# A state-space layer on one core: decay factors from running sums spread by transfers, in place of products with a triangle, and x rows turned last in their slots

## The chip, the cores and the metric

One Trainium2 chip, one of its cores. The time is that of one execution on the device, in microseconds (us); several runs are made and their median is given. Smaller is better.

## What is computed

A stack of layers on 256 positions of width 1024, float32: SwiGLU blocks, a state-space (Mamba-2) mixer, latent attention, a gated short convolution and a stick-breaking attention. The change is in the state-space mixer, which runs once. Its core, with chunks of 128 positions, 8 groups and 4 heads per group:

```python
acs = jnp.cumsum(dtc * a, axis=1)
seg = acs[:, :, None] - acs[:, None, :]
decay = jnp.exp(jnp.where(mask, seg, -jnp.inf))
cb = jnp.einsum("blgn,bsgn->blsg", cc, bc)
xdt = xc * dtc[..., None]
y_diag = jnp.einsum("blsg,blsgr,bsgrp->blgrp", cb, decay, xdt)
y_off = jnp.einsum("blgn,bgrpn->blgrp", cc, state) * jnp.exp(acs)[..., None]
decay_to_end = jnp.exp(acs[:, -1:] - acs)
```

`dt` is a softplus of a projection, `a` is negative, `xc`, `bc` and `cc` come from a projection, a causal convolution over four positions and a SiLU.

## The kernel before

The kernel is one program with a hand-written order for each of the five engines; semaphores tie them together. Every matrix product with weights is made of three products of split operands (`product`, L622 to L624: high by high, high by low, low by high, in fp32r). Weights come in units of 512 KB x 2 through a ring of four: SyncE loads `raw` (L510), ScalarE rounds it to `w_hi` (L1367), the vector engine (DVE) forms `w_lo = raw - w_hi` (L1974), and TensorE waits for `lo_ready` ahead of each unit's first product.

In the state-space layer (`mamba` of each engine) TensorE goes through 22 units of the input projection, two per step `s`, 0 to 10. Behind unit number n comes **slot n**: a batch of small work of the scan, listed by `mamba_slots(n)`. In this text slot 14, say, is the batch behind the unit of that number. Its entries, for group g:

- `dt`, `acs`: time steps; running sums of `dA = dt * a` (product with the triangle `upto`), slot 8.
- `xs` (slots 12, 14, 16, 18): a quarter of x is transposed in two turns (L639) and copied by ScalarE to `ys` (L1548).
- `cb` (from slot 12): products of B and C (L915), and for g - 2 the product of C with the carried state (L909). DVE takes `off` (L2182) and `cbm`, the masked product (L2190).
- `seg` (from slot 12): for both chunks the differences of running sums, as a product of the triangle `after_r` with `dA` spread over `upto`, in a high part `R_hi` (ScalarE, L1578, eight ACTIVATEs a group) and a low part `R_lo` (POOL, L2691). TensorE writes them to the PSUM tile `aux` (L924, L925); ScalarE takes `dend` (L1558) and the exponentials `E` (L1559); DVE multiplies E by `cbm` (L2206).
- `y` (from slot 13): E by `xdt`, eight products (L933), added to `ys` by DVE (L2211). `xdt` and `xdtd` are POOL's (L2700, L2710).
- `state` (from slot 13): B by `xdtd` (L943), copied by ScalarE (L1562).

Results of `xs`, `cb`, `y` and `state` share one PSUM tile, `tr`, with two buffers. Each use takes a **turn** number k from a common counter, and `claim_turn(k)` on TensorE waits until turn k - 2 has been read (`turn_done`, `turn_free`). A slot takes 2 turns for `xs`, 1 for `cb`, 1 for `y` and 1 for `state`. In slots with `xs`, TensorE and ScalarE do them in the order xs, seg, cb, y, state; in others cb, y, seg, state. Each engine goes through its own part of the slot in program order, then splits the next weight unit (`split_to`). ScalarE also does `first_tap` and `finish_conv` (the convolution's start and its SiLU, L1591, L1605) and DVE the rest of the convolution (`taps`, L2245), up to step 7. Exp and SiLU need different activation tables (ACT_TABLE_LOAD rows).

Of the kernel before, what the change touches and what calls it, by code (L numbers as in the profile page):

```python
# [20 lines left out]
P = 128  # L21
# [90 lines left out]
MAMBA_TURNS = {"dt": 1, "acs": 1, "btok": 1, "xs": TB, "cb": 1, "y": 2, "seg": 0, "state": 0, "g": TB}  # L112
# [52 lines left out]
def mamba_slots(n, sums_first=False):  # L165
# [11 lines left out]
    if n in (12, 14, 16, 18):  # L177
        found.append(("xs", (n - 12) // 2))
# [36 lines left out]
def program(nc, t, out):  # L215
# [4 lines left out]
    with ctx:  # L220
# [6 lines left out]
        def overlaid(*specs):  # L227
# [4 lines left out]

        raw = sb("raw", [P, RING, UNIT])
# [12 lines left out]
        after_r = sb("after_r", [P, P], F32R)  # L246
# [25 lines left out]
        BT, CT, Btok, conv, E, xdt, R_hi, R_lo, cbm, xdtd, state, dtT = overlaid(  # L272
            ("BT", [P, G, T], F32), ("CT", [P, G, T], F32), ("Btok", [P, G, P], F32),
            ("conv", [P, 4, T], F32), ("E", [P, TB, R * P], F32), ("xdt", [P, 2, TB, GW], F32),
            ("R_hi", [P, TB, R * P], F32R), ("R_lo", [P, TB, R * P], F32R), ("cbm", [P, TB, P], F32),
# [14 lines left out]
        (sz, _, ys, xsT, off, dtv, dta, dte, dt, ea, dA, dA_hi, dA_lo, eacs, dend, gss, gms, grs, sz0) = overlaid(  # L290
# [3 lines left out]
            ("dA", [P, TB, NH], F32), ("dA_hi", [P, TB, NH], F32R), ("dA_lo", [P, TB, NH], F32),  # L294
            ("eacs", [P, NH], F32), ("dend", [P, R], F32), ("gss", [P, TB, G], F32),
# [19 lines left out]
        (_, rows, after, causal, strict) = overlaid(  # L315
            ("_junk2", [P, 2 * D], F32), ("rows", [P, 4, P], F32), ("after", [P, P], F32),
# [29 lines left out]
        consts = sem("consts")  # L346
        gated = sem("gated")
# [16 lines left out]
        r_ready = sem("r_ready")  # L364
        r_hi_ready = sem("r_hi_ready")
# [38 lines left out]
        after_ready = sem("after_ready")  # L404
# [212 lines left out]
        def _(pe):  # L617
# [228 lines left out]
            def mamba():  # L846
                pe.wait_ge(consts, 9)
                pe.wait_ge(after_ready, 1)
# [28 lines left out]
                def small(n, only=None):  # L877
                    for name, g in mamba_slots(n, True):
# [1955 lines left out]
```

## Time and profile before

| | |
|---|---|
| median of 3 runs | 1298.96 us (1298.92 to 1299.41) |
| the profiled execution | 1299.49 us, its span 1297.8 us |
| TensorE busy | 1277.3 us, 98% |
| DVE, ScalarE, POOL busy | 59%, 53%, 9% |
| DMA | 219.81 MB, mean 169 GB/s |
| slots 12 to 20 of the state-space layer | 289.5 to 370.9 us of the span |

A profile row gives engine, line, operation, output and inputs by the program's names, count, and time. A product in float32 shows as two passes (x2 for one product); one in fp32r as one. "Idle before" is time that the engine stood still ahead of an instruction, with what released it. The chain of waits follows the last instruction back through whatever released it, so its pieces are time on the path. PE is TensorE, PEld its weight load, ACT ScalarE, POOL GpSimd; ACTq and SPq are the issue of DMAs on those engines.

### The profile page before, as it was taken

How to read it: one execution, taken by the hardware profiler on the slowest of the kernel's cores; microseconds unless marked ns; L12 is line 12 of the kernel's file. 1: busy time of each engine (PE TensorE's matmuls, PEld its weight loads, DVE VectorE, ACT ScalarE, POOL GpSimd, SP SyncE). 2: the span in 40 equal slices, each digit the busy share in tenths (PEclk: the TensorE clock that was granted, in tenths of full speed). 3: DMA queues.
4: the chain of work that ended last, by engine and by line, in shares of the span. 5: the costliest groups of instructions: out<-in, count | busy, mean ns of one | idle time of the engine just before them, and what ended most of it. 6: DMA issues, size and time to landing. Idle time of an engine off the chain costs nothing.

```text
span 1297.8 us, 18319 instructions
## 1 busy us (share of the span) xinstructions
PE 1277.3 (98%) x6934; PEld 1094.6 (84%) x6934; DVE 763.6 (59%) x892; ACT 682.2 (53%) x924; POOL 122.3 (9%) x198
## 2 busy tenths in 40 slices
PE   8999999999999999999999999989999999999997
PEld 7888889999888888888888888877888888999896
DVE  5655645878795655554555545765655554666654
ACT  6544435669883644443544534854644443444554
POOL 3000000008730000000000001620000000000000
PEclk9999999999999999999999999999999999999999
DMA  9656646453246466555655463412566565565431
GB/s 300 206 183 209 218 144 195 145 181 98 98 163 219 137 194 194 186 203 163 194 180 180 175 227 110 161 54 79 193 194 192 193 213 162 148 192 182 147 114 49
DMA packets 180653, 219.81 MB, mean 169 GB/s; under 512 B 8713, under 2 KB 132942, under 8 KB 180590
## 3 DMA queue, kind: packets, MB, share of 16 engines
q1 hardware_dynamic: 179614, 218.01, 51.8%
q8 instruction: 42, 0.69, 0.2%
q10 hardware_dynamic: 688, 0.79, 0.2%
q14 instruction: 21, 0.17, 0.1%
q0 software_dynamic: 288, 0.15, 0.0%
HBM read 217.87 MB, written 1.05 MB: 169 GB/s over the span
## 4 chain that ended last, share of the span: by engine, by line
PE 89%; ACT 4%; DVE 4%; issue 1%; DMA 1%; SPq 1%; POOL 1%; DVEq 0%; POOLq 0%; ACTq 0%
PE acc L622 27%; PE acc L624 27%; PE acc L623 27%; PE tr L639 4%; DVE w_lo L1974 1%; ACT w_hi L1367 1%; PE tr L933 1%; DMA raw<-in_ffn_w_up 1%; PE aux L1075 1%; PE acc L1056 1%; ACT xT_hi L1379 0%; ACT R_hi L1578 0%; ACT junk L1433 0%; SPq L510 0%; PE aux L924 0%
## 5 line engine op out<-in xcount | busy, mean ns | idle before, releaser
L1974 DVE TENSOR_TENSOR w_lo<-raw,w_hi 128x2048 fp32r<-128x2048 f32 (+2 forms) x187 | 420.4, 2275 | 176.4 <-ACT w_hi L1367 176.2
L1367 ACT ACTIVATE w_hi<-raw 128x2048 fp32r<-128x2048 f32 (+2 forms) x189 | 352.1, 1897 | 118.0 <-PE acc L624 117.2
L622 PE MATMUL acc<-w_hi,xT_hi 128*128 128x512 f32 (+1 forms) x914 | 362.4, 396 | 0.7 <-DVE w_lo L2594 0.4
L624 PE MATMUL acc<-w_hi,xT_lo 128*128 128x512 f32 (+1 forms) x914 | 355.1, 388 | 0.0
L623 PE MATMUL acc<-w_lo,xT_hi 128*128 128x512 f32 (+1 forms) x914 | 354.2, 388 | 0.0
L624 PEld LDWEIGHTS acc<-w_hi,xT_lo 128*128 128x128 f32 x914 | 171.6, 188 | 36.2
L622 PEld LDWEIGHTS acc<-w_hi,xT_hi 128*128 128x128 f32 x914 | 171.8, 188 | 35.8 <-issue 1.6
L623 PEld LDWEIGHTS acc<-w_lo,xT_hi 128*128 128x128 f32 x914 | 172.0, 188 | 33.0
L622 PE MATMUL acc<-w_hi,hT_hi 128*128 128x512 f32 x448 | 176.0, 393 | 0.4 <-DVE y_sb L2494 0.4
L624 PE MATMUL acc<-w_hi,hT_lo 128*128 128x512 f32 x448 | 174.5, 389 | 0.0
L623 PE MATMUL acc<-w_lo,hT_hi 128*128 128x512 f32 x448 | 174.4, 389 | 0.0
L622 PE MATMUL acc<-xT_hi,w_hi 128*128 128x256 f32 (+1 forms) x592 | 167.2, 283 | 1.2 <-DVE w_lo L1974 0.6
L623 PE MATMUL acc<-xT_lo,w_hi 128*128 128x256 f32 (+1 forms) x592 | 165.9, 281 | 0.0
L624 PE MATMUL acc<-xT_hi,w_lo 128*128 128x256 f32 (+1 forms) x592 | 165.9, 281 | 0.0
L2116 DVE SCALAR_TENSOR_TENSOR h<-acc,rstd,sg 128x256 f32<-128x256 f32 x88 | 38.6, 479 | 163.9 <-ACT sg L1481 163.9
L1481 ACT ACTIVATE sg<-acc,rstd 128x256 f32<-128x256 f32 x88 | 37.0, 472 | 180.1 <-PE acc L624 180.1
L622 PEld LDWEIGHTS acc<-xT_hi,w_hi 128*128 128x128 f32 (+1 forms) x592 | 112.2, 190 | 1.9 <-issue 1.7
L623 PEld LDWEIGHTS acc<-xT_lo,w_hi 128*128 128x128 f32 (+1 forms) x592 | 112.3, 190 | 0.2
L624 PEld LDWEIGHTS acc<-xT_hi,w_lo 128*128 128x128 f32 (+1 forms) x592 | 112.3, 190 | 0.0
L2666 POOL TENSOR_SCALAR mean_square<-square_sum 128x1 f32<-128x1 f32 x18 | 4.9, 275 | 1026.8 <-ACT junk L1433 567.3
L624 PEld LDWEIGHTS acc<-w_hi,hT_lo 128*128 128x128 f32 x448 | 84.1, 188 | 17.8
L622 PEld LDWEIGHTS acc<-w_hi,hT_hi 128*128 128x128 f32 x448 | 84.1, 188 | 17.7 <-DVE y_sb L2494 0.8
(298 smaller groups left out, 1160.4 us busy)
## 6 DMA issues: line engine op xcount, KB each, us to landing
raw<-in_ffn_w_down SPq DMA_DIRECT2D x88, 512.0 KB, 4.9
raw<-in_ffn_w_gate SPq DMA_DIRECT2D x86, 512.0 KB, 4.2
raw<-in_ffn_w_up SPq DMA_DIRECT2D x86, 512.0 KB, 5.2
raw<-in_ssm_w_in SPq DMA_DIRECT2D x48, 512.0 KB, 4.6
raw<-in_w_in_a SPq DMA_DIRECT2D x64, 256.0 KB, 4.1
raw<-in_ssm_w_out SPq DMA_DIRECT2D x16, 512.0 KB, 4.0
raw<-in_mla_w_out SPq DMA_DIRECT2D x8, 512.0 KB, 4.4
raw<-in_w_out_a SPq DMA_DIRECT2D x8, 512.0 KB, 5.0
```

The lines of the kernel that those rows point to most:

```text
L622: pe.matmul(o, lh, rh, start=start, stop=False, skip_group_check=skip)
L623: pe.matmul(o, lh, rl, start=False, stop=False, skip_group_check=skip)
L624: return pe.matmul(o, ll, rh, start=False, stop=stop, skip_group_check=skip)
L639: last = pe.transpose(tr[0:n, k % 2, at:at + P], src, ident[:])
L933: last = pe.matmul(tr[:, k % 2, tb * GW + r * HP:tb * GW + (r + 1) * HP], E[:, tb, r * P:(r + 1) * P], xdt[:, g % 2, tb, r * HP:(r + 1) * ...
L1056: pe.matmul(o[:, j * w:(j + 1) * w], qT[0:QK, h0 + j, tb * P:(tb + 1) * P], kT[0:QK, h0 + j, 0:w], start=j == 0, stop=False, skip_group_ch ...
L1075: last = pe.matmul(aux[:, r % 2, j * (VD + 1):(j + 1) * (VD + 1)], pT[:, r % 2, at:at + P], kv_tok[:, kb, h0 + j, NOPE:], start=kb == 0, s ...
L1367: inst = act.activation(w_hi[:, u % RING, 0:n], raw[:, u % RING, 0:n], ACT.Copy)
L1481: act.activation(sg[:, tb, :], bank(p0 + n, tb)[:, 0:CW], ACT.Silu, scale=rstd[:, tb:tb + 1]).then_inc(gated, 1)
L1974: inst = dve.tensor_tensor(w_lo[:, u % RING, 0:n], raw[:, u % RING, 0:n], w_hi[:, u % RING, 0:n].bitcast(F32), ALU.subtract)
L2116: acc_free(dve.scalar_tensor_tensor(h[:, tb, :], bank(p0 + n, tb)[:, CW:2 * CW], rstd[:, tb:tb + 1], sg[:, tb, :], ALU.mult, ALU.mult), p0 ...
L2666: link(pool.tensor_scalar(mean_square[:, b], square_sum[:, at:at + 1], 1.0 / D, EPS, ALU.mult, ALU.add))
```

## The change

`dA` no longer goes through products with a triangle. In slot 8, `acs` forms with TensorE, in one turn: the running sums of both chunks by position (128x64), the same transposed with heads on partitions (two products, 32x128), and minus the sum from a position to the chunk's end (two products, 128x32). ScalarE takes from it `eacs`, `dend` for all heads at once, `nacs` (the negated sums) and `dtT`, 32 rows of 256 sums, which it sends to DRAM (`decay_rows`, 32 KB). Per group a DMA on ScalarE's queue spreads four of the rows over all 128 partitions into one of three buffers of `E` (512 KB, `sum_rows`): groups 0 and 1 ahead of slot 10's share of the convolution, group g + 2 in slot g + 12, from g = 1 to 5 behind `y(g-1)`, which read that buffer. POOL adds the mask `future` (0 or a large negative number, `segments`), ScalarE takes eight exponentials of 128 columns with the bias `nacs`, and DVE multiplies by `cbm` as before. Precision splits of `dA`, `R_hi`, `R_lo` and the use of `aux` here are gone. `xs` stands last in its slot on all engines, so that in a slot the turns go to cb, y, state, xs, xs.

```diff
-    if n in (12, 14, 16, 18):
-        found.append(("xs", (n - 12) // 2))
...
-    for name, first in (("y", 13), ("seg", 12), ("state", 13)):
+    for name, first in (("y", 13), ("decay", 12), ("state", 13)):
         if 0 <= n - first < G:
             found.append((name, n - first))
-    if sums_first and found and found[0][0] == "xs":
-        found.sort(key=lambda slot: ("xs", "seg", "cb", "y", "state").index(slot[0]))
+    if n in (12, 14, 16, 18):
+        found.append(("xs", (n - 12) // 2))
...
+        decay_rows = nc.dram_tensor("decay_rows", (NH, T), F32).ap()
-        after_r = sb("after_r", [P, P], F32R)
+        future = sb("future", [P, P])
...
-            ("conv", [P, 4, T], F32), ("E", [P, TB, R * P], F32), ("xdt", [P, 2, TB, GW], F32),
-            ("R_hi", [P, TB, R * P], F32R), ("R_lo", [P, TB, R * P], F32R), ("cbm", [P, TB, P], F32),
+            ("conv", [P, 4, T], F32), ("E", [P, 3, R, T], F32), ("xdt", [P, 2, TB, GW], F32),
+            ("cbm", [P, TB, P], F32),
...
                         elif name == "acs":
                             pe.wait_ge(dt_dve, 2)
                             claim_turn(k)
-                            pe.matmul(tr[:, k % 2, 0:NH], upto[:], dA[:, 1, :], start=True, stop=True)\
+                            pe.matmul(tr[:, k % 2, 0:TB * NH], upto[:], dA[:].rearrange("p b n -> p (b n)"),
+                                      start=True, stop=True)
+                            for tb in range(TB):
+                                pe.matmul(tr[0:NH, k % 2, (tb + 1) * P:(tb + 2) * P], dA[:, tb, :], upto[:],
+                                          start=True, stop=True)
+                            end = tr[:, k % 2, (TB + 1) * P:(TB + 1) * P + NH]
+                            pe.matmul(end, ones[:], dA[:, 0, :], start=True, stop=False, skip_group_check=True)
+                            pe.matmul(end, upto[:], dA[:, 0, :], start=False, stop=True, skip_group_check=True)\
                                 .then_inc(turned, 1)
...
-                        elif name == "seg":
-                            for tb in range(TB):
-                                pe.wait_ge(r_hi_ready, 2 * g + tb + 1)
-                                pe.wait_ge(r_ready, 2 * g + tb + 1)
-                                if g:
-                                    pe.wait_ge(exp_done, 2 * g + tb - 1)
-                                pe.matmul(aux[:, tb, :], after_r[:], R_hi[:, tb, :], start=True, stop=False)
-                                pe.matmul(aux[:, tb, :], after_r[:], R_lo[:, tb, :], start=False, stop=True)\
-                                    .then_inc(seg_ready, 1)
...
+                def sum_rows(g):
+                    act.dma_start(E[:, g % 3, :, :].rearrange("p r t -> p (r t)"),
+                                  across(decay_rows[R * g:R * g + R, :].rearrange("r t -> (r t)"), R * T))\
+                        .then_inc(sums_landed[g % 3], 16)
...
                         if name == "acs":
                             act.wait_ge(turned, k + 1)
-                            turn_free(act.activation(eacs[:], tr[:, k % 2, 0:NH], ACT.Exp), k)
+                            act.activation(eacs[:], tr[:, k % 2, NH:2 * NH], ACT.Exp)
+                            act.activation(dend[:], tr[:, k % 2, (TB + 1) * P:(TB + 1) * P + NH], ACT.Exp, scale=-1.0)
+                            sums = tr[:, k % 2, 0:TB * NH].rearrange("p (b n) -> p b n", b=TB)
+                            act.activation(nacs[:], sums, ACT.Copy, scale=-1.0)
+                            turn_free(act.activation(dtT[0:NH, :], tr[0:NH, k % 2, P:P + T], ACT.Copy), k)
+                            turn_done(act, k)
+                            act.dma_start(decay_rows[:, :], dtT[0:NH, :]).then_inc(sums_stored, 16)
...
-                        elif name == "seg":
-                            if n in (14, 16, 18):
-                                act.wait_ge(turned, c.turn + 2)
+                        elif name == "decay":
+                            if g + 2 < G:
+                                if g:
+                                    act.wait_ge(turned, ky[0] + 1)
+                                sum_rows(g + 2)
                             for tb in range(TB):
                                 act.wait_ge(seg_ready, 2 * g + tb + 1)
-                                if tb == 0:
-                                    act.activation(dend[:], aux[:, 0, P - 1::P], ACT.Exp)
-                                act.activation(E[:, tb, :], aux[:, tb, :], ACT.Exp).then_inc(exp_done, 1)
+                                for r in range(R):
+                                    e = E[:, g % 3, r, tb * P:(tb + 1) * P]
+                                    inst = act.activation(e, e, ACT.Exp, bias=nacs[:, tb, R * g + r:R * g + r + 1])
+                                inst.then_inc(exp_done, 1)
+                        elif name == "y":
+                            ky[0] = k
...
-                def high_factors(g):
...
-                        for r in range(R):
-                            inst = act.activation(R_hi[:, tb, r * P:(r + 1) * P], upto[:], ACT.Copy,
-                                                  scale=dA_hi[:, tb, R * g + r:R * g + r + 1].bitcast(F32))
...
-                    if 6 <= s < 10:
-                        high_factors(2 * s - 11)
+                    if s == 5:
+                        act.wait_ge(sums_stored, 16)
+                        sum_rows(0)
+                        sum_rows(1)
...
-                        elif name == "seg":
...
-                                pool.tensor_tensor(
-                                    heads(R_lo[:, tb, :], R), upto[:].unsqueeze(1).to_broadcast([P, R, P]),
-                                    dA_lo[:, tb, R * g:R * g + R].unsqueeze(2).to_broadcast([P, R, P]), ALU.mult)\
-                                    .then_inc(r_ready, 1)
...
-                            pool.wait_ge(exp_done, 2 * g + 1)
...
+                def segments(g):
+                    pool.wait_ge(sums_landed[g % 3], 16 * (g // 3 + 1))
+                    for tb in range(TB):
+                        e = E[:, g % 3, :, tb * P:(tb + 1) * P]
+                        inst = pool.tensor_tensor(e, e, future[:].unsqueeze(1).to_broadcast([P, R, P]), ALU.add)
+                        inst.then_inc(seg_ready, 1)
...
                 for n in range(22):
+                    if n == 11:
+                        segments(0)
                     small(n)
+                    if 12 <= n < 11 + G:
+                        segments(n - 11)
```

TensorE, slot 14 of the input projection, before, from the second transpose of x on (`tr_read0` and `tr_read1` are the releases of the two buffers of `tr`):

```order
L639 MATMUL tr<-ident,xsT 128x128 x3
L639 MATMUL tr<-ident,xsT 128x128 [waits tr_read0]
L639 MATMUL tr<-ident,xsT 128x128 x3
L924 MATMUL aux<-R_hi,after_r 128x512 [waits exp_done,r_ready,r_hi_ready]
L925 MATMUL aux<-R_lo,after_r 128x512
L924 MATMUL aux<-R_hi,after_r 128x512 [waits exp_done,r_ready,r_hi_ready]
L925 MATMUL aux<-R_lo,after_r 128x512
L909 MATMUL tr<-state,CT 128x256 [waits tr_read0,tr_read1]
L915 MATMUL tr<-CT,BT 128x128 x2
L933 MATMUL tr<-xdt,E 128x64 [waits m_ready,xdt_ready,tr_read0]
L933 MATMUL tr<-xdt,E 128x64 x7
L943 MATMUL tr<-xdtd,Btok 128x256 [waits xdtd_ready,tr_read1]
```

The x transposes and the products into `aux` come first. TensorE, the same slot, now:

```order
L916 MATMUL tr<-state,CT 128x256 [waits tr_read0,tr_read1]
L922 MATMUL tr<-CT,BT 128x128 x2
L931 MATMUL tr<-xdt,E 128x64 [waits m_ready,xdt_ready,tr_read0]
L931 MATMUL tr<-xdt,E 128x64 x7
L941 MATMUL tr<-xdtd,Btok 128x256 [waits xdtd_ready,tr_read1]
L639 MATMUL tr<-ident,xsT 128x128 [waits tr_read0,conv_done]
L639 MATMUL tr<-ident,xsT 128x128 x3
L639 MATMUL tr<-ident,xsT 128x128 [waits tr_read1]
L639 MATMUL tr<-ident,xsT 128x128 x3
L622 MATMUL acc<-xT_hi,w_hi 128x256 [waits lo_ready]
```

The four products into `aux` are gone, and the two x turns stand behind `state`; the second waits for the release of the buffer that `state` wrote. (L909 is now L916, L915 L922, L933 L931, L943 L941.)

ScalarE, slot 14 and the split of the weight unit behind it, before:

```order
L1548 ACTIVATE ys<-tr 128x512 [waits turned] x2
L1605 ACT_TABLE_LOAD
L1605 ACTIVATE xsT<-conv 128x512 [waits acc_read2]
L1605 ACTIVATE xsT<-conv 128x512 [waits acc_read3]
L1558 ACT_TABLE_LOAD [waits seg_ready]
L1558 ACTIVATE dend<-aux 128x4 [waits turned]
L1559 ACTIVATE E<-aux 128x512
L1559 ACTIVATE E<-aux 128x512 [waits seg_ready]
L1562 ACTIVATE state<-tr 128x256 [waits turned]
L1367 ACTIVATE w_hi<-raw 128x2048 [waits unit_used,raw_landed0]
```

Here the x copies and the SiLU of the convolution come first. ScalarE, the same place, now:

```order
L1533 DMA E<-decay_rows 128x1024 [waits turned]
L1570 ACTIVATE E<-E,nacs 128x128 [waits seg_ready]
L1570 ACTIVATE E<-E,nacs 128x128 x3
L1570 ACTIVATE E<-E,nacs 128x128 [waits seg_ready]
L1570 ACTIVATE E<-E,nacs 128x128 x3
L1576 ACTIVATE state<-tr 128x256 [waits turned]
L1557 ACTIVATE ys<-tr 128x512 [waits turned] x2
L1607 ACT_TABLE_LOAD
L1607 ACTIVATE xsT<-conv 128x512 [waits acc_read2]
L1607 ACTIVATE xsT<-conv 128x512 [waits acc_read3]
L1365 ACTIVATE w_hi<-raw 128x2048 [waits unit_used,raw_landed0]
```

The copy of `state` now has a DMA issue and eight exponentials in front of it, and the x copies, `xsT` and `w_hi` come behind it.

## Rows read from the trace of the kernel before

**Rows 1.** The page's first parts: busy time of TensorE, its granted clock in 40 slices.
```profile
PE 1277.3 (98%) x6934; PEld 1094.6 (84%) x6934; DVE 763.6 (59%) x892; ACT 682.2 (53%) x924; POOL 122.3 (9%) x198
...
PEclk9999999999999999999999999999999999999999
```

**Rows 2.** The chain of waits, slot 14 and the next slot's start: start us, us, what.
```profile
306.82 0.87 PE tr L639 x8
307.70 0.23 PE aux L924
...
308.62 0.43 PE tr L909 x2
...
309.50 1.73 PE tr L933 x16
311.23 0.49 PE tr L943 x2
317.47 0.43 PE tr L909 x2
```

**Rows 3.** The tile `aux`: engine, operation, count, ns min/median/max, starts, forms.
```profile
L924 PE MATMUL aux<-R_hi,after_r x16: 393/471/497, 290.1 to 361.9; 128*128 128x512 f32 x16
```

**Rows 4.** Who waited for whom, 215 to 385 us: total, times, longest us.
```profile
PEld aux L924 <- ACT R_hi L1578: 1.8, 1, 1.8
```

**Rows 5.** The chain of waits on ScalarE ahead of slot 18, from `state`.
```profile
344.28 0.27 ACT state L1562
344.56 1.80 ACT w_hi L1367
346.36 2.32 ACT R_hi L1578 x8
```

**Rows 6.** Timeline of TensorE at `acs`: start us, us, engine, line, operation, count.
```profile
266.06 0.30 PE L893 MATMUL tr<-dA,upto 128*128 128x32 f32 x2
```

**Rows 7.** Timeline of ScalarE around slot 12.
```profile
290.93 1.15 ACT L1605 ACTIVATE xsT<-conv 128x512 f32<-128x512 f32 x2
292.10 1.28 ACT L1558 ACT_TABLE_LOAD   x1
293.39 0.17 ACT L1558 ACTIVATE dend<-aux 128x4 f32<-128x4 f32 x1
293.46 1.08 ACT L1559 ACTIVATE E<-aux 128x512 f32<-128x512 f32 x2
```

**Rows 8.** Timeline of ScalarE's queue at the program's start.
```profile
1.25 1.00 ACTq L484 DMA_DIRECT2D raw<-in_ffn_w_up  x2
```

**Rows 9.** Timeline of DVE, slots 13, 14 and 16; [idle before it <- releaser].
```profile
296.66 3.12 DVE L1974 TENSOR_TENSOR w_lo<-raw,w_hi 128x2048 fp32r<-128x2048 f32 x1
299.71 0.41 DVE L2190 TENSOR_TENSOR cbm<-tr,upto 128x256 f32<-128x256 f32 x1
...
306.64 2.28 DVE L1974 TENSOR_TENSOR w_lo<-raw,w_hi 128x2048 fp32r<-128x2048 f32 x1
309.54 0.42 DVE L2182 TENSOR_TENSOR off<-tr,eacs 128x256 f32<-128x256 f32 x1 [0.61 <-PE tr L915]
...
311.27 0.69 DVE L2211 TENSOR_TENSOR ys<-tr,ys 128x512 f32<-128x512 f32 x1 [0.33 <-PE tr L933]
...
333.20 2.55 DVE L2206 TENSOR_TENSOR E<-E,cbm 128x512 f32<-128x512 f32 x2
```

**Rows 10.** DMA issues: tensors, queue, count, KB each, us to landing.
```profile
in_gain<-in_norm_a SPq DMA_DIRECT2D x1, 512.0 KB, 7.0
f_gain<-in_norm_f SPq DMA_DIRECT2D x1, 512.0 KB, 3.8
```

**Rows 11.** Timeline of POOL, slots 13, 14 and 17.
```profile
302.75 2.04 POOL L2691 TENSOR_TENSOR R_lo<-upto,dA_lo 128x512 fp32r<-128x512 f32 x2
308.53 0.86 POOL L2700 TENSOR_TENSOR xdt<-ys,dt 128x256 f32<-128x256 f32 x1 [3.74 <-ACT ys L1548]
...
344.95 4.63 POOL L2691 TENSOR_TENSOR R_lo<-upto,dA_lo 128x512 fp32r<-128x512 f32 x2
```

More of the change, by code:

```diff
@@ L108, in unscaled @@
     return name[:3] == "ffn" or name == "mla"
-MAMBA_TURNS = {"dt": 1, "acs": 1, "btok": 1, "xs": TB, "cb": 1, "y": 2, "seg": 0, "state": 0, "g": TB}
+MAMBA_TURNS = {"dt": 1, "acs": 1, "btok": 1, "xs": TB, "cb": 1, "y": 2, "decay": 0, "state": 0, "g": TB}
 SMALLS = 16 * 9
@@ L271, in program @@
         hT_hi, hT_lo = overlaid(("hT_hi", [P, KF, T], F32R), ("hT_lo", [P, KF, T], F32R))
-        BT, CT, Btok, conv, E, xdt, R_hi, R_lo, cbm, xdtd, state, dtT = overlaid(
+        BT, CT, Btok, conv, E, xdt, cbm, xdtd, state, dtT = overlaid(
             ("BT", [P, G, T], F32), ("CT", [P, G, T], F32), ("Btok", [P, G, P], F32),
-            ("conv", [P, 4, T], F32), ("E", [P, TB, R * P], F32), ("xdt", [P, 2, TB, GW], F32),
-            ("R_hi", [P, TB, R * P], F32R), ("R_lo", [P, TB, R * P], F32R), ("cbm", [P, TB, P], F32),
+            ("conv", [P, 4, T], F32), ("E", [P, 3, R, T], F32), ("xdt", [P, 2, TB, GW], F32),
+            ("cbm", [P, TB, P], F32),
             ("xdtd", [P, GW], F32), ("state", [P, GW], F32), ("dtT", [P, T], F32))
@@ L289, in program @@
                                    ("junk", [P, D], F32), ("xn", [P, TB, D], F32))
-        (sz, _, ys, xsT, off, dtv, dta, dte, dt, ea, dA, dA_hi, dA_lo, eacs, dend, gss, gms, grs, sz0) = overlaid(
+        (sz, _, ys, xsT, off, dtv, dta, dte, dt, ea, dA, nacs, eacs, dend, gss, gms, grs, sz0) = overlaid(
             ("sz", [P, TB, 512], F32), ("_junk", [P, D], F32), ("ys", [P, TB, DI], F32),
@@ L314, in program @@
         _, in_gain = overlaid(("_g1", [P, 6 * D], F32), ("in_gain", [P, D], F32))
-        (_, rows, after, causal, strict) = overlaid(
-            ("_junk2", [P, 2 * D], F32), ("rows", [P, 4, P], F32), ("after", [P, P], F32),
+        (_, rows, causal, strict) = overlaid(
+            ("_junk2", [P, 2 * D], F32), ("rows", [P, 4, P], F32),
             ("causal", [P, P], F32), ("strict", [P, P], F32))
@@ L363, in program @@
         dt_act = sem("dt_act")
-        r_ready = sem("r_ready")
-        r_hi_ready = sem("r_hi_ready")
+        sums_copied = sem("sums_copied")
+        sums_stored = sem("sums_stored")
+        sums_landed = [sem(f"sums_landed{n}") for n in range(3)]
         seg_ready = sem("seg_ready")
@@ L877, in small @@
                 def small(n, only=None):
-                    for name, g in mamba_slots(n, True):
+                    for name, g in mamba_slots(n):
                         if only and name != only:
@@ L1939, in rotation @@
                 act.activation(causal_b[:], causal[:], ACT.Copy)
-                act.activation(strict_b[:], strict[:], ACT.Copy)
-                act.activation(after_r[:], after[:], ACT.Copy).then_inc(after_ready, 1)
+                act.activation(strict_b[:], strict[:], ACT.Copy).then_inc(masks_ready, 1)
             first_x(act, 0, 0)
@@ L2638, in _ @@
             select(from_[:], 0, 1, -1, ALU.is_ge, -1.0, 0.0)
-            select(after[:], 0, 1, -1, ALU.is_gt, 1.0, 0.0)
+            select(future[:], 0, -1, 1, ALU.is_ge, 0.0, NEG)
             pool.memset(ones[:], -1.0).then_inc(consts, 1)
@@ L2684, in small @@
                             xs_turn[g] = k
-                        elif name == "seg":
-                            if g == 0:
-                                pool.wait_ge(dt_dve, 3)
-                            for tb in range(TB):
-                                if g:
-                                    pool.wait_ge(seg_ready, 2 * g + tb - 1)
-                                pool.tensor_tensor(
-                                    heads(R_lo[:, tb, :], R), upto[:].unsqueeze(1).to_broadcast([P, R, P]),
-                                    dA_lo[:, tb, R * g:R * g + R].unsqueeze(2).to_broadcast([P, R, P]), ALU.mult)\
-                                    .then_inc(r_ready, 1)
+                        elif name == "acs":
+                            acs_turn.append(k)
                         elif name == "y":
```

34 lines of the change are left out of this document (12 added, 22 removed).

## The prediction

> **What bounds the kernel now.** I read the page first: TensorE is busy for 98% of the span, and in the 40 slices its granted clock is at the top digit throughout, the 2.4 GHz level [rows 1]. So a product taken off TensorE shortens the kernel, unless another engine's wait takes its place. The profiled run took 1299.49 us and the median of the runs is 1298.96, 0.5 lower; I make the sum against 1299.49 and take the same off the median. A measurement of this kernel tells about 0.2%, 2.6 us, from no change.
>
> Next the chain of waits through the state-space stage. Slot 14 (306.8 to 311.7 us) is TensorE without a gap [rows 2]: eight transposes of x 0.87, two pairs of `after_r` products at 0.23 each, the `cb` products 0.88 from 308.62 to 309.50, `y` 1.73, `state` 0.49. The `after_r` products are what goes. There are 16 with `R_hi` [rows 3] and, in pairs with them, 16 with `R_lo`, 32 in all. The only time in this stage when TensorE stands still is 1.8 us in slot 18, waiting for ScalarE's `R_hi` [rows 4]. Over slots 16 to 18 ScalarE is thus the late engine; what it does in its last slot before the wait is `state` 0.27, `w_hi` 1.80, eight `R_hi` 2.32 [rows 5].
>
> **The change, part by part.**
>
> Removed on TensorE: 32 products at 0.23 us on the path [rows 2, 3]: -7.4. Removed with them: the wait for `R_hi`, -1.8 [rows 4]. What is late next in slot 18 is below.
>
> Added on TensorE in `acs` (slot 8): four more products than the one of before. One product shows there as two passes [rows 6], and `y` (eight products) makes 16 passes in 1.73 us, 0.108 each [rows 2]; eight more passes are +0.9. They wait for nothing new. Bounds: 0.4 (half of that, as most of these passes are narrower in weights) to 1.8 (0.23 each, as a wide product).
>
> ScalarE, per group: two exponentials of 512 columns, `dend`, and eight `R_hi` of 128 go; eight exponentials of 128 with a bias per partition come. Before, no exponential of that shape is to be seen. The nearest row is `R_hi`, same shape and one operand per partition: 2.32 for eight [rows 5]. I take that. Bounds: 1.1 (the time of the two wide ones, [rows 7]) to 4.3 (eight at the 0.54 of a wide one, [rows 7]). ScalarE gains about 1 us per group and loses a DMA issue of 0.5 us for six of the eight [rows 8].
>
> DVE loses one small subtraction; its product with `cbm` has the same 512 columns. POOL's `R_lo`, 2.0 us a group, or 4.6 beside DVE [rows 11], becomes the addition of `future`, also two SBUF operands and 512 columns: no change in length. It moves earlier, a slot ahead of its use. The start of the program swaps one mask for another and drops one copy, hidden behind the first units: 0.
>
> The transfers: 512 KB each from one 4 KB row of DRAM, as `f_gain` and `in_gain`, which land after 3.8 and 7.0 us [rows 10]. `sum_rows(g+2)` is issued in slot g+12 behind `y(g-1)`. Behind POOL's addition for g+2 stands its `xdt` for g+1, which `y(g+1)` in slot g+14 needs. For E(4): issued 3.2 us after slot 14 began; `y(3)` is wanted at 21.5 by the reckoning below; the two additions take at most 4.6 and the four `xdt` and `ys` products 3.4 at 0.86 each [rows 11]. That leaves 21.5 - 4.6 - 3.4 - 3.2 = 10.3 us for the landing. So 0 for all eight, and for the 32 KB store in slot 8, read first in slot 10. SP issues nothing of this, so no weight load stands behind it.
>
> **The new wait, worked out.** The x transposes now stand last in the slot and take turns k+3 and k+4, where `cb` has k, `y` k+1, `state` k+2. A turn needs its buffer's last reader: the first x turn needs DVE's `ys` of `y`, the second needs ScalarE's copy of `state`. And ScalarE reaches that copy only after: `y(g-1)` done, DMA issue 0.5, eight exponentials 2.3, copy 0.3, [rows 5, 8], 3.2 with the hand-overs. TensorE covers of that only `state` 0.49 and one x turn 0.44 [rows 2]. It stands still for 3.2 - 0.9 = 2.3 us in slot 14 and again in slot 16. In slots 12 and 18 it is different:
> - Slot 12 has no `y`; the second x turn needs DVE's `cbm`, 0.4 us, behind 0.44 of x turns: +0.1.
> - Slot 18 (g = 6) issues no DMA and doesn't wait for `y(5)`, so the exponentials come early. But by the same reckoning ScalarE's `w_hi` lets DVE start `w_lo` (2.3, [rows 9]) only 0.5 us before `cb` is done, and DVE comes to `off` and `cbm` 1.8 after it; `state` needs `cb` read, the first x turn needs `ys` (0.4, 0.4, 0.7 and an addition that I take at 0.3, [rows 9]). From `cb`, that is 3.6 us against the 1.73 + 0.49 = 2.2 that TensorE has before the x turn: +1.4 at most, +0.3 if DVE is ahead. I take +1.2.
> - Slots 13 and 15: DVE's row from `cbm` to the end of the product with E is 6.9 us in slot 13 [rows 9]. Before, E is ready 2.9 us ahead of `y` in slot 14 (DVE turns to `w_lo` at 306.6, `y` starts at 309.5, [rows 2, 9]). Now TensorE reaches `y` sooner by the pairs removed in slots 13 and 14 and by the x turns behind it (0.9 + 0.9 + 0.9), 2.7 in all, so nothing or a tenth remains; and `state` in slot 13 waits a few tenths for `cbm` behind a long `w_lo`. For all three +0.4, from 0 to 1.
>
> Sum: -7.4 - 1.8 + 0.9 + 0.1 + 0.4 + 2.3 + 2.3 + 1.2 = **-2.0 us**. Profiled 1297.5, median 1297.0.
>
> **Weights.** The new order also delays ScalarE's next `w_hi`: in even slots it now stands behind the x copies, which come at the slot's end. For the unit after slot 15, reckoned from the start of slot 14: `state` copied at 5.8, x copies done 6.9 (0.54 each, as an E of that shape, [rows 7]), table load 8.2, `xsT` 9.4 [rows 7], `w_hi` 11.2 [rows 5], `w_lo` 13.6 [rows 9]. TensorE: slot 14 takes 0.9 + 1.7 + 0.5 + 0.9 + 2.3 = 6.3, the unit 5.8 (311.7 to 317.5, [rows 2]), slot 15 3.1, so it wants the half at 15.1. Covered, by 1.5 us. (Slot 16 comes a unit later, at 20.6, its `y` at 21.5.) For the unit after slot 13 the same reckoning leaves 0.7, with `w_lo` at its long 3.1 [rows 9].
>
> **A rule against the change.** In slot 12 the exponentials now come before `xsT`, which adds a switch to Exp and one back there. A load takes 1.28 us, and the next instruction starts 1.29 after the load did (292.10 to 293.39, [rows 7]). I used that. The Trainium skill (ScalarE: Activation LUTs, What ACT_TABLE_LOAD costs) puts each switch at 2.66 us, the load and a drain of 1.38. By that `w_hi` for the unit after slot 13 would come 2.8 us later, TensorE would wait 2.1, and the sum would be +0.1. The row speaks against it: no drain shows.
>
> **The rivals.**
> 1. *Only the two waits of slots 14 and 16.* The small terms (0.1, 0.4, 1.2) vanish because DVE is ahead, and `acs` costs 0.4: -9.2 + 0.4 + 4.6 = -4.2, 1294.8. With the exponentials at their lower bound too, 1.2 less in each slot: -6.6, 1292.4. For it: DVE sits idle in slot 14 for 0.6 us before `off` and 0.3 before `ys` [rows 9]. Against: DVE's order, by which `w_lo` stands ahead of `cbm`. Chance 0.22.
> 2. *Slower: the weight halves.* TensorE waits for `lo_ready` after slots 13, 15 and 17. Place: ScalarE's `w_hi` behind the x copies, then DVE's `w_lo`. It decides from 1.5 us more than my reckoning (0.7 in slot 13). `w_lo` is 3.12 beside POOL's work against 2.28 in the next slot, the E product 2.55 against 1.28 [rows 9], and POOL's additions now run at other times. With both at their long times, 2.1 us more, and 0.9 of hand-overs that I left out, TensorE waits 1.5 to 2.3 us behind each of slots 13, 15 and 17, some +6 over the forecast: 1303. Chance 0.15.
> 3. *No gain: the waits move.* ScalarE and DVE bound slots 12 to 18 altogether, and the products removed were filling a pace that these engines set. Then the stage ends when it did, -0.5 to +0.5: 1299.0. For it: before slot 18 TensorE waited for ScalarE, which worked without a gap [rows 4, 5]. Against: ScalarE's work shrinks by about 1 us per group. Chance 0.15.
> 4. *Table loads at twice their time*: a switch of 2.6 us in place of 1.3, so -2.0 plus 2.1, +0.1, 1299.1. Against it the one row that shows it. Chance 0.02.
>
> **How the numbers follow.** My forecast has 0.46, and its own range, from the bounds of its terms, is 1295.5 to 1298.5. It straddles the line of 0.2% (1296.4): 0.16 of its chance is faster, 0.30 the same. Rival 1 gives 0.21 faster, 0.01 same; rival 2 gives 0.13 slower and 0.02 same; rival 3 0.13 same and 0.02 slower; rival 4 same. Faster 0.37, same 0.48, slower 0.15. The range of 1293.0 to 1300.5 leaves out most of rival 2 and the end of rival 1.
>
> **What the profile after would show.** `aux` is not written in this stage. TensorE waits about 2.3 us before an x transpose in slots 14 and 16, released by ScalarE's `state` copy; 1 us or so in slot 18; no wait for `E` or `R_hi`. Eight exponentials take 2.3 us. POOL's addition never waits for a landing after slot 13 in a way that delays `xdt`. The forecast is wrong if those two waits are under 1 us, if `w_lo` releases TensorE in this stage for more than 1 us in all, or if anything outside slots 8 to 20 changes by over 1 us.

## The result, and the profile after

The changed kernel takes **1303.13 us** (1300.67 to 1305.72, 10 runs) against 1298.94 (1298.35 to 1299.52, 10 runs) before: a ratio of 1.003, interval 1.0021 to 1.0039, slower by 4.2 us. The prediction was 1297.0, with a range up to 1300.5. The profiled run took 1303.7 us with a span of 1302.0 (before 1299.49 and 1297.8).

The page after, the lines that answer to [rows 1]:

```profile
PE 1275.2 (98%) x6910; PEld 1092.9 (84%) x6910; DVE 761.3 (58%) x891; ACT 675.0 (52%) x901; POOL 134.1 (10%) x198
...
PEclk9999999998999999999999999999999999999999
```

TensorE has 24 instructions fewer and is busy for 2.1 us less, and the kernel is longer all the same. One slice, the tenth (293 to 325 us), shows a granted clock of 8 where all were 9. The reader looks there for two things: a wait, and what it does to the clock. Who waited for whom on TensorE, 215 to 400 us, answers to [rows 4]:

```profile
PE tr L941 <- DVE cbm L2189: 4.1, 3, 1.7
PE tr L639 <- DVE ys L2210: 2.2, 3, 0.7
```

Three slots, two waits in each: `state` (L941) for DVE's `cbm`, and the first transpose of x (L639) for DVE's `ys`. ScalarE releases nothing. TensorE in slot 14, beside [rows 2]:

```profile
307.73 1.73 PE L931 MATMUL tr<-xdt,E 128*128 128x64 f32 x14
310.93 0.70 PE L941 MATMUL tr<-xdtd,Btok 128*128 128x256 f32 x2 [1.48 <-DVE cbm L2189]
312.37 1.94 PE L639 MATMUL tr<-ident,xsT 128*128 128x128 f32 x8 [0.74 <-DVE ys L2210]
313.96 0.56 PE L622 MATMUL acc<-xT_hi,w_hi 128*128 128x256 f32 x1
```

From here I count from one start to the next, with what lies between: `y` with the wait behind it takes 3.37 (before 1.74), `state` with its wait 1.44 (0.30), the transposes 1.59 (0.79). The last holds no wait, and neither does the weight unit behind it: 7.81 where it was 5.94. The clock in those microseconds (columns: stretch; its length; busy us and count of PE, PEld, DVE, ACT, POOL; granted clock; DMA share; GB/s):

```profile
311.00:312.00 1.00, 0.63 (x2) 0.23 (x2) 1.00 (x2) 1.00 (x5) 0.34 (x1) 0.82 0.95 307
312.00:313.00 1.00, 0.63 (x3) 0.66 (x4) 1.00 (x3) 0.58 (x3) 0.00 (x0) 0.50 0.64 141
...
317.00:318.00 1.00, 1.00 (x7) 1.00 (x7) 0.00 (x0) 1.00 (x2) 0.95 (x2) 0.50 0.00 0
318.00:319.00 1.00, 1.00 (x8) 1.00 (x8) 0.00 (x0) 1.00 (x1) 1.00 (x2) 0.77 0.00 0
```

0.50 of full speed is the 1.2 GHz level. The clock fell between the start of `state` and the end of the second wait and came back nearly 7 us later, while TensorE worked on at half speed. In slot 16 the same from 335.5 to 338.9 us: transposes 1.59, unit 6.10 for 5.68. In slot 18, where the first wait was 0.92 and the second 0.74, the transposes took 0.82: no fall. The Trainium skill (TensorE: Matmul & The Clock Gate, Part 1: The HAM clock gate) says that a gate sets the array's clock by how busy the engine has recently been, at 1.2 or 2.4 GHz; the trace agrees with both levels.

Why DVE was late: its timeline in slot 14, beside [rows 9], and POOL's, beside [rows 11]:

```profile
306.86 3.35 DVE L1975 TENSOR_TENSOR w_lo<-raw,w_hi 128x2048 fp32r<-128x2048 f32 x1
310.13 0.41 DVE L2181 TENSOR_TENSOR off<-tr,eacs 128x256 f32<-128x256 f32 x1
310.47 0.41 DVE L2189 TENSOR_TENSOR cbm<-tr,upto 128x256 f32<-128x256 f32 x1
310.91 0.71 DVE L2195 TENSOR_TENSOR ys<-ys,off 128x256 f32<-128x256 f32 x1
311.55 0.68 DVE L2210 TENSOR_TENSOR ys<-tr,ys 128x512 f32<-128x512 f32 x1
```

```profile
306.69 1.38 POOL L2708 TENSOR_TENSOR E<-E,future 128x512 f32<-128x512 f32 x1 [2.45 <-DMA E<-decay_rows]
308.02 3.32 POOL L2708 TENSOR_TENSOR E<-E,future 128x512 f32<-128x512 f32 x1
...
318.19 1.30 POOL L2708 TENSOR_TENSOR E<-E,future 128x512 f32<-128x512 f32 x1
319.44 3.33 POOL L2708 TENSOR_TENSOR E<-E,future 128x512 f32<-128x512 f32 x1
```

Before, x and the four products into `aux` opened the slot (1.80 us, 306.66 to 308.46), `w_lo` took 2.28, and DVE then had to wait 0.61 for `cb` [rows 9]. Now `cb` is done at 307.56 and DVE gets to it at 310.13. POOL does two additions beside it, and `w_lo` takes 3.35. The next `w_lo` has two additions beside it as well, and takes 2.39:

```profile
319.24 2.39 DVE L1975 TENSOR_TENSOR w_lo<-raw,w_hi 128x2048 fp32r<-128x2048 f32 x1 [5.82 <-ACT w_hi L1365]
362.81 2.29 DVE L1975 TENSOR_TENSOR w_lo<-raw,w_hi 128x2048 fp32r<-128x2048 f32 x1 [2.37 <-ACT w_hi L1365]
```

The last line is a `w_lo` with no addition under way. What differs is how long the first addition, already under way when `w_lo` began, went on: 1.20 us in slot 14 (306.86 to 308.06), 0.25 in the next. Slot 16 has 1.13 and `w_lo` 3.28; the `w_lo` at 352.94 has 0.38 and 2.54. So in these rows `w_lo` grows by about the time that it shares with an addition begun before it. An addition begun after it costs it next to nothing and is itself drawn out to 3.3 us, from 1.3. In slot 14 its start was set by the landing of its transfer, for which POOL stood idle for 2.45 us. (The Trainium skill, GPSIMD Engine Reference, Key points, says that POOL shares its SBUF interfaces with VectorE and contends with VectorE's instructions that have two SBUF inputs. `w_lo` is one, and the trace agrees: 3.35 against 2.29 at 362.81, where no addition was under way.)

### The profile page after: what moved, and what is told of

Same layout as the page of the kernel before. It is cut to its first block, busy times and chain, and to the rows that moved or that the text cites. A ratio compares the mean times of both kernels' runs of the same rounds, so it can differ in the third digit from the quotient of the medians.

```text
span 1302.0 us, 18231 instructions
## 1 busy us (share of the span) xinstructions
PE 1275.2 (98%) x6910; PEld 1092.9 (84%) x6910; DVE 761.3 (58%) x891; ACT 675.0 (52%) x901; POOL 134.1 (10%) x198
## 3 DMA queue, kind: packets, MB, share of 16 engines
q10 hardware_dynamic: 1888, 5.01, 1.1%
## 4 chain that ended last, share of the span: by engine, by line
PE 87%; DVE 6%; ACT 3%; issue 2%; DMA 1%; SPq 1%; POOL 0%; ACTq 0%; DVEq 0%; POOLq 0%
PE acc L622 27%; PE acc L624 27%; PE acc L623 27%; PE tr L639 4%; DVE w_lo L1975 2%; ACT w_hi L1365 1%; DVE conv L2244 1%; DMA raw<-in_ffn_w_up 1%; PE aux L1073 1%; PE acc L1054 1%; ACT xT_hi L1377 0%; ACT junk L1431 0%; SPq L510 0%; PE tr L931 0%; SPq L484 0%
```

## The experiments

Each was timed in five rounds beside the kernel before on the same chip. The first four ask whether the order of x or the pace of the other engines costs the time, what the releaser is, and what the clock costs.

**e1_x_first.** The change with x first in its slots, as before.

```diff
+    if n in (12, 14, 16, 18):
+        found.append(("xs", (n - 12) // 2))
     for name, first in (("y", 13), ("decay", 12), ("state", 13)):
...
-    if n in (12, 14, 16, 18):
-        found.append(("xs", (n - 12) // 2))
```

> The changed kernel with the x transposes first in their slots again, on all engines; the decay chain stays as changed. Theory A (the x transposes at the slot's end make TensorE wait for turns, and the waits let its clock fall): no wait over 1 us in slots 14 and 16, no stretch at half clock, 1290 to 1294 us, that is 1298.9 less 7.4 for the products, less 1.8 for the wait for R_hi, plus 1.3 for the sums of slot 8. Theory B (the decay chain itself, its POOL additions and transfers, makes DVE late and TensorE wait): waits of 1 us or more stay in slots 14 and 16, 1298 us or more.

Measured: 1299.72 (before 1299.16), ratio 1.0002, interval 0.9993 to 1.0011. Of the 4.2 us of loss 3.4 come from x's place. Neither theory came whole: no wait of 1 us stands in slots 14 and 16 and the clock holds in this stage, as theory A has it, but the time is theory B's, and with x first and 32 products fewer there is still no gain. TensorE's waits:

```profile
PE tr L941 <- DVE cbm L2189: 2.5, 4, 0.9
PE tr L916 <- ACT ys L1557: 0.8, 3, 0.3
PE tr L931 <- DVE E L2205: 0.5, 1, 0.5
```

The waits for `cbm` now stand in slots 13, 15 and 17, a shorter one in slot 16. In the first three, before, two pairs of `aux` products (1.01 us from start to start) stood between `y` and `state`, just where DVE needed time for `cbm` behind `w_lo`. Slots 13, 15 and 17 take 2.86, 2.79 and 2.36 us for `y` and its wait, instead of 1.7 and 1.0 of products. The products had been cover. These rows are from a run of 1297.99 us, 1.7 under the median, and seven of the eleven runs took 1299.4 or more; they show the waits, not all of the time.

**e2_products_x_last.** The kernel before with x last in its slots, and without the wait by which ScalarE let both x turns come first. The edit moves the products into `aux` too: in slots 14, 16 and 18 they stood ahead of `cb` and now stand between `y` and `state`, as in the other slots.

```diff
-    if n in (12, 14, 16, 18):
-        found.append(("xs", (n - 12) // 2))
...
-    if sums_first and found and found[0][0] == "xs":
-        found.sort(key=lambda slot: ("xs", "seg", "cb", "y", "state").index(slot[0]))
+    if n in (12, 14, 16, 18):
+        found.append(("xs", (n - 12) // 2))
...
-                            if n in (14, 16, 18):
-                                act.wait_ge(turned, c.turn + 2)
```

> The kernel before, products with the triangle kept, with the x transposes moved to the end of their slots on all engines. Theory A: TensorE waits before state or x transposes in slots 14 and 16, 2 us or more each, and its clock falls there: 1302 to 1308 us. Theory B: the order alone costs nothing, 1297 to 1300 us.

Measured: 1300.01 (before 1299.16), ratio 1.0006, interval 0.9997 to 1.0016. Theory A's 1302 and more is missed. The waits:

```profile
PE tr L637 <- DVE ys L2207: 0.5, 1, 0.5
PE tr L637 <- ACT state L1558: 0.4, 2, 0.2
PE aux L922 <- issue: 0.2, 1, 0.2
```

Putting x last costs 3.4 us in the change (1303.13 less 1299.72) and at most 0.9 here, which isn't clear of noise; here the products stand between `y` and `state`, just where the change waits for `cbm`. It takes both parts of the change together to uncover DVE.

**e3_state_copy_early.** The change, with ScalarE's copy of `state` in front of the DMA issue and the exponentials: the step on which the forecast rested.

```diff
-                    for name, g in mamba_slots(n):
+                    for name, g in sorted(mamba_slots(n), key=lambda slot: ("cb", "y", "state", "decay", "xs").index(slot[0]) if n >= 12 and n < 21 else 0):
```

> The changed kernel with ScalarE's copy of the state ahead of the DMA issue and the exponentials in each slot. The forecast's step (ScalarE's copy releases the second x turn, 2.3 us a slot): the waits of slots 14 and 16 shrink to under 1 us, the clock holds, 1295 to 1298 us. As the profile after reads (DVE's cbm and ys, late behind w_lo, release TensorE): waits of 1.5 and 0.7 us stay, 1301 to 1304 us.

Measured: 1304.75 (before 1299.16), ratio 1.0045, interval 1.0031 to 1.0059. Taking away the forecast's releaser gains nothing; slot 14 has the same two stretches (3.38 and 1.43 us for 3.37 and 1.44), and the wait for `off` is new:

```profile
PE tr L941 <- DVE cbm L2189: 4.0, 4, 1.5
PE tr L639 <- DVE ys L2210: 1.5, 3, 0.7
PE tr L941 <- DVE off L2181: 1.1, 1, 1.1
```

**e4_waits_filled.** The change, with idle products in slots 14, 16 and 18: six ahead of `state`, three behind it, into an accumulator that nothing reads.

```diff
+                def fill(n, count):
+                    if n in (14, 16, 18):
+                        for _ in range(count):
+                            pe.matmul(aux[:, 0, 0:P], upto[:], ident[:], start=True, stop=True)
```

> The changed kernel with idle products (128x128 float32 into the unused tile aux, 6 behind y and 3 behind state, in slots 14, 16 and 18) that keep TensorE busy during its waits; nothing reads them. If the fall of the clock behind the waits costs time: no stretch at half clock, 1297.5 to 1300 us and little scatter. If the half clock costs nothing by itself (the weights or DVE set the pace anyway): 1302 to 1305 us, as without them.

Measured: 1299.78 (before 1299.16), ratio 1.0005, interval 0.9996 to 1.0014. DVE is about as late as in the change, but TensorE works meanwhile: from `y`'s start to the transposes' the three slots take 4.81, 4.30 and 4.23 us, in the change 4.81, 5.01 and 4.25. The stretch 311 to 319 us, of the change and of this kernel:

```profile
311.00:319.00 8.00, 7.26 (x35) 6.89 (x36) 2.43 (x4) 6.80 (x12) 4.09 (x7) 0.57 0.56 179
```

```profile
311.00:319.00 8.00, 7.92 (x66) 7.71 (x65) 2.99 (x4) 6.68 (x11) 5.36 (x7) 1.00 0.45 154
```

In these 8 us TensorE does 66 instructions, a few of them idle, instead of 35, at a clock of 1.00 instead of 0.57. Work that nothing needs makes the kernel 3.35 us faster (1303.13 less 1299.78): that is what the fallen clock costs. The single runs of the change say it too: 1300.67 us at a mean clock of 0.997, 1305.72 at 0.992.

What is left is DVE's pace. The next four ask how much of it is POOL, and e8 how much comes from late weight halves.

**e5_no_additions** and **e6_x_first_no_additions**. The change, and e1, without POOL's additions of `future`; the exponentials take 0.001 of the sums and one bias per head, so the mask and the true decay factors are left out. ScalarE then waits for the transfer itself (`sums_landed`) instead of for POOL, so that hand-over goes as well.

```diff
-                                    inst = act.activation(e, e, ACT.Exp, bias=nacs[:, tb, R * g + r:R * g + r + 1])
+                                    inst = act.activation(e, e, ACT.Exp, scale=0.001,
+                                                          bias=eacs[:, R * g + r:R * g + r + 1])
...
-                    if 12 <= n < 11 + G:
-                        segments(n - 11)
```

> The changed kernel, x transposes last, without POOL's 16 additions of the mask; so that nothing overflows, the exponentials take 0.001 of the sums and another bias, so the decay factors and the mask are left out of the result. If POOL's additions slow DVE (w_lo 3.3 us beside them against 2.3, the E product likewise) and DVE's lateness at cbm is what TensorE waits for: the waits of slots 14 and 16 shrink to under 1 us each, the clock holds, 1295 to 1299 us. If DVE's order alone makes it late: waits and half clock stay, 1301 to 1304 us.

> The x transposes first and no additions (the decay factors and the mask left out of the result, as in e5). Theory C (with the products gone DVE sets the pace, and the additions beside it are a part of its time): waits for cbm and E under 0.5 us in all but one slot, 1294 to 1297 us. If the additions don't matter: as e1, 1299 to 1300 us.

Measured: e5 1301.0 (before 1299.18), ratio 1.0013, interval 1.0004 to 1.0022; e6 1296.97, ratio 0.9984, interval 0.9975 to 0.9993. The additions cost 2.1 us with x last (1303.13 less 1301.0) and 2.8 with x first (1299.72 less 1296.97); the kernel before is within 0.3 us in all these calls, and the intervals on either side of each difference just touch, so both numbers are loose. DVE's `w_lo` between 288 and 370 us, in the change and in e5:

```profile
L1975 DVE TENSOR_TENSOR w_lo<-raw,w_hi 128x2048 fp32r<-128x2048 f32 x7 | 18.6, 2662 | 18.1 <-ACT w_hi L1365 18.1
```

```profile
L1976 DVE TENSOR_TENSOR w_lo<-raw,w_hi 128x2048 fp32r<-128x2048 f32 x8 | 18.7, 2332 | 19.9 <-ACT w_hi L1365 19.9
```

0.33 us of each `w_lo` on average, most of it in slots 14 and 16. And e5's waits:

```profile
PE tr L639 <- ACT state L1577: 1.8, 2, 1.1
PE tr L941 <- DVE cbm L2190: 1.8, 3, 0.7
PE tr L639 <- DVE ys L2211: 1.4, 3, 0.5
```

Here is the forecast's wait for ScalarE's copy of `state`: it was real, but hidden behind the longer one for DVE, and shows when that shrinks. The clock, however, didn't hold, as the expectation had it. In e5's profiled run, of 1302.59 us, it falls as in the change:

```profile
311.00:319.00 8.00, 7.14 (x37) 7.14 (x38) 1.88 (x3) 6.12 (x9) 5.01 (x8) 0.57 0.41 158
```

So without POOL's additions the other waits are still enough for the fall, and the time, 1301.0, is that of the expectation's other reading, DVE's order alone; of the 4.2 us the additions explain about half. In e6 the clock holds in this stage, but the expectation's mark, waits under 0.5 us in all but one slot, is missed: 2.4 us for `cbm` in three, the longest 1.1, where e1 has 2.5 in four.

**e7_x_first_mask_by_select.** x first, and the mask put on by one select over the addresses in place of an addition of a second tile. It computes all that the reference asks.

```diff
-                        inst = pool.tensor_tensor(e, e, future[:].unsqueeze(1).to_broadcast([P, R, P]), ALU.add)
+                        inst = pool.affine_select(out=e, in_=e, compare_op=ALU.is_ge, fill=NEG, base=0,
+                                                  pattern=[[0, R], [1, P]], channel_multiplier=-1)
```

> The x transposes first and the mask set by POOL's affine_select in place, with one input from SBUF where the addition has two; the result is the full one. If it is the second input that makes DVE and POOL slow each other: w_lo beside it 2.3 us, 1296 to 1298.5 us. If a select costs POOL and DVE as much as the addition, or more: 1299 us or more.

Measured: 1296.99 (before 1299.18), ratio 0.9981, interval 0.9972 to 0.999: faster than both kernels, as fast as e6, which has no masking at all. POOL's masking between 288 and 370 us, in the change, in e1 and in e7:

```profile
L2708 POOL TENSOR_TENSOR E<-E,future 128x512 f32<-128x512 f32 x13 | 30.0, 2329 | 6.5 <-DMA E<-decay_rows 6.5
```

```profile
L2708 POOL TENSOR_TENSOR E<-E,future 128x512 f32<-128x512 f32 x13 | 23.5, 1829 | 6.9 <-DMA E<-decay_rows 6.9
```

```profile
L2708 POOL TENSOR_SCALAR_AFFINE_SELECT E<-E 128x512 f32<-128x512 f32 x12 | 14.2, 1204 | 11.2 <-DMA E<-decay_rows 11.2
```

On DVE it is the product with `cbm` that gets shorter, in e1 and in e7:

```profile
L2205 DVE TENSOR_TENSOR E<-E,cbm 128x512 f32<-128x512 f32 x16 | 15.0, 966 | 6.4 <-ACT E L1570 6.4
L2205 DVE TENSOR_TENSOR E<-E,cbm 128x512 f32<-128x512 f32 x16 | 11.6, 745 | 6.8 <-ACT E L1570 6.8
```

`w_lo` hardly does (2.43 us to 2.37), and TensorE's waits for `cbm` are 2.4 us in three, as in e6. That the select gains 2.7 us over e1 is shown by the times; through which wait it does so is not. Nor is it shown that the second input matters and not the length: alone, an addition takes 1.30 us and a select 0.63.

**e8_x_first_early_splits.** e1 with the weights' two halves made one place earlier on ScalarE and DVE in this stage, so that `w_hi` and `w_lo` don't come late.

```diff
-                    if s < 6 or s == 10:
-                        split_to(u0 + 2 * s + 3)
+                    split_to(u0 + 2 * s + 3)
...
-                    split_to(u0 + 2 * s + (4 if s < 6 else 3))
+                    split_to(u0 + 2 * s + 4)
```

(DVE's two calls are edited alike.)

> The x transposes first and, on ScalarE and DVE, the splits of the weight units of steps 6 to 9 one place earlier, as in the steps before. If DVE is late in slot 13 because w_lo waits for ScalarE's w_hi (3 us idle ahead of the E product in e1): the wait for cbm in slot 13 goes, 1297.5 to 1299 us. If DVE's whole load sets the pace: as e1, 1299 to 1300.5 us.

Measured: 1300.3 (before 1299.18), ratio 1.0012, interval 1.0003 to 1.0022. The waits for `cbm` are still there (2.8 us in four, 2.5 in e1), slot 13 takes the same 2.86 us for `y` and its wait, that for `E` grows from 0.5 to 0.9, one of 0.8 for `off` is new, and in the profiled run the clock fell in slot 13. Earlier halves don't make DVE early. The expectation's other reading, that DVE's whole load sets the pace, fits the time; the edit moves `w_hi` and `w_lo` together and doesn't show it.

**e9_x_last_mask_by_select.** The change as it stands, with e7's select.

> The change with x's transposes last in their slots, as it stands, and with GpSimd's masking of the decay rows done by a select in place of the addition of a triangle. Theory A (the loss is VectorE's queue: the weights' low half runs beside the additions and holds up the products that `state` and x wait for): the waits at `state` (8.8 us in three) and at x (2.2 us in three) shrink, the clock falls in fewer slots, and the time is 1298 to 1301. Theory B (the order of x is what costs, whatever GpSimd does): the waits stay above 3 us in all, the clock still falls in slot 14 or 16, and the time is 1301.5 to 1303.5.

Measured: 1299.76 (before 1299.32), ratio 1.0002, interval 0.9993 to 1.0011. (The 8.8 us of the expectation isn't TensorE's wait at `state`; its row has 4.1.) The time is theory A's. Of its marks only one came: the waits shrink from 6.3 us to 4.5, but the clock still falls in both slots, as theory B has it, in slot 14 for a shorter time (0.79 over 311 to 319 us, where the change has 0.57), in slot 16 for the same (0.76 over 333 to 340 in both):

```profile
PE tr L941 <- DVE cbm L2189: 2.9, 3, 1.1
PE tr L639 <- DVE ys L2210: 0.9, 2, 0.5
PE tr L639 <- ACT state L1576: 0.7, 1, 0.7
```

With e1 and e7 this makes a square, each as its distance from the kernel before in its own call: addition and x last +4.2, addition and x first +0.6, select and x last +0.4, select and x first -2.2. Each of the two is worth about 3 us (2.6 to 3.8), whichever way the other stands.

**e10_x_first_select_filled.** e7 with e4's `fill` for slots 13, 15 and 17, called once, ahead of `state`: `+ fill(n, 4)`.

> The change with x first and the mask by a select, and in slots 13, 15 and 17 four idle products of 128 columns (into the spare accumulator that nothing reads) between y and `state`, where TensorE waits for VectorE's products of C and B. Theory A (in some executions these waits lower TensorE's clock, which is the spread from 1295.8 to 1300.2 of the version without them): no stretch at half clock, a spread under 2 us, and a median of 1295.5 to 1296.5. Theory B (the spread has another cause): a spread as before and a median of 1297 to 1298.5, since the idle products only lengthen slots where nothing was waited for.

Measured: 1296.77 (1295.88 to 1298.95; before 1299.32), ratio 0.9982, interval 0.9973 to 0.9991. Neither theory: the median didn't move, and the spread went from 4.4 us to 3.1. In the profiled run of e7 the clock fell behind a wait of 1.12 us in slot 13 (unit 7.33 us), in that of e10 not in this stage. The two runs are 4.3 us apart. Start against start, 1.9 us of it arises behind that fall, and 1.7 behind another at 848 to 854 us, in the attention layer, which no edit here touches and where the kernel before, too, has a shorter one. So a part of the spread comes from outside the stage, and the fill can't take it away. One run of each is no proof; what sets e10's two runs 2 us above its median isn't shown.

## Why the prediction was wrong

The terms of the sum, as the prediction has them, against the profiled run of after; each measured one is the difference from start to start between the two timelines:

| term | forecast | measured |
|---|---|---|
| 32 products gone | -7.4 | -8.1 (8 slots at 1.01) |
| wait for `R_hi` gone | -1.8 | -1.6 |
| `acs` | +0.9 | +1.15 |
| slot 12 | +0.1 | +0.4 |
| slots 13 and 15 | +0.4 | +0.2 |
| slots 14, 16, 18, waits | +2.3, +2.3, +1.2 | +2.8, +3.0, +2.2 |
| clock at 1.2 GHz, slots 14 and 16 | not in the sum | +2.7, +1.2 |
| ahead of slot 8 | 0 | +0.4 |
| sum | -2.0 | +4.35; by the spans +4.2 |

- **What failed first is a term that was not there.** The forecast read the clock as the top digit throughout and kept it there, without a reason, while it put 2.3 us of idle time into slots of 5 us. TensorE then ran transposes and a weight unit at half the rate: 0.80 and 1.87 us in slot 14, 0.80 and 0.42 in slot 16, 3.9 in all. Filling the waits takes 3.35 of it away (e4). Without this term the difference is +0.3, and the time would have lain in the range, though not at the forecast. (The page's digits hide short falls: the kernel before, too, has 0.50 from 850 to 852 us, in another layer.)
- **"The new wait, worked out" has the wrong releaser.** It had ScalarE's copy of `state` release the second x turn. It was DVE: `cbm` for `state`, then `ys` for the first x turn. Its own sign of being wrong, those waits under 1 us, came: x waited 0.74 us in each slot, and `state` 1.48, 1.67 and 0.92, where the forecast had no wait in slots 14 and 16. The forecast had DVE's chain (`w_lo`, `off`, `cbm`, `ys`) but reckoned it for slot 18 alone, with `w_lo` at 2.3 and the addition ahead of `ys` at 0.3 (2.54 and 0.71 there). For slots 14 and 16 it named DVE's `ys` and gave it no time; the row where DVE *waited* for `cb` [rows 9] comes in only for rival 1, as if DVE would go on being early when the 1.8 us of work ahead of `cb` went away. In slot 14 `w_lo` came 0.2 us later and took 1.1 longer. So the three slots cost 8.0 us and not 5.8. e3 takes the forecast's releaser away and gains nothing; e5 shows that it stands next.
- **POOL's addition: "no change in length".** R_lo had a mean of 1.54 us between 288 and 370, the addition 2.33. The prediction had the right row for the worst case, 4.63 for two beside DVE [rows 11], but put it on POOL's account alone. It counts on DVE's too, where it was on the path: 1.07 and 1.00 us of `w_lo` in slots 14 and 16, by the mean 0.33 of each, and about 2.1 us of the kernel (e5). That the spreading DMA held the addition back by 2.45 us in slot 14, into the time of `w_lo`, is seen in the rows; that an earlier landing would have kept them apart wasn't tried.
- **Rival 3 was nearest in its mechanism** (products removed had been filling a pace that others set), at a chance of 0.15, and e1 is its case: +0.6 us, no gain from 32 products fewer. Of the engines that it names DVE was the main one: of e1's 4.0 us of waits ScalarE's copies of x hold 1.0. **Rival 2** has the time, 1303, but not the mechanism: TensorE never waited for `lo_ready` in this stage. What it says of `w_lo` (3.12 beside POOL's work against 2.28) is what came about, one step further on. **Rival 1** fell: DVE's terms grew.
- **Rival 4 and its rule.** The table load at 287.28 us takes 1.28 and the first exponential starts at 288.58, as in [rows 7]. The 2.66 of the Trainium skill (ScalarE: Activation LUTs, What ACT_TABLE_LOAD costs) shows in neither kernel.
- What held: eight exponentials take 2.45 us for the 2.3 taken, the DMA issue 0.33 for 0.5; `y` never waits for `E`, and the landings (median 5.5 us) delay no `xdt` for which TensorE waits; nothing outside slots 8 to 20 moved by 1 us.

## What to carry to other kernels

Work taken off the bounding engine is a gain only where nobody was using its time: ahead of each place that you shorten, look up what the other engines finish under it, above all an engine whose row shows a short idle gap there (it is early by that much and no more). A wait on TensorE can cost more than its length: price it once as idle time and once as what follows at half clock, and where it can't be avoided, put other work into it. And when an elementwise operation moves on POOL, look at which DVE instruction will start while it runs: here the one that came second bore the delay. The shorter form, the select, was the cheaper one for both engines.

## What the runs showed of the hardware

- Two waits of 1.48 and 0.74 us, with only `state` between them, brought the granted clock to 0.50 for nearly 7 us; 1.67 and 0.74 us in slot 16 did it for 3.4 us, 0.92 and 0.74 in slot 18 not at all. In e9 it fell behind one of 1.12 us in slot 16, in e7 behind one of 1.12 in slot 13; in e6 one of 1.11 in the same slot 13 and in e8 one of 1.22 in slot 16 passed without a fall. So waits of about 1 us put it at risk; they don't settle it.
- DVE's `w_lo` and POOL's additions in the change: where an addition was under way for the first 1.20 and 1.13 us of `w_lo`, `w_lo` took 3.35 and 3.28 us; for 0.25, 2.39 (three times); for 0.38, 2.54; for none, 2.29. The addition begun beside a running `w_lo` took 3.3 us each time, one with only the convolution beside it 1.30.
- A select with one tile as input, 128x512 on POOL: 1.20 us in e7 and 1.02 in e9. The addition of a second tile, same shape: 1.83 in e1 and 2.33 in the change. These are means; with neither `w_lo` nor the product with `cbm` beside them a select took 0.63 and an addition 1.30.
- A row of 4 KB in DRAM spread over 128 partitions (512 KB), behind one issue of 0.33 us on ScalarE's queue, lands after a median of 5.5 us beside the weight stream.
